# Two output products ended row tile by row tile, and the last layer's input turned, split and first multiplied by tiles

## The reference

```python
def even_layer(x, ...):                    # first layer of the second block
    ...
    y = jnp.concatenate([y_a, y_b], axis=-1) @ w_out        # 256x2048 @ 2048x1024
    return x + rms_norm_2(y, g_post)

def odd_layer(x, ...):                     # last layer
    h = rms_norm_2(x, g_pre)
    p = h @ w_in                                            # 256x1024 @ 1024x2752
    c_q, c_kv, k_r, f_in, z_c, z_d = split_cols(p, ODD_SIZES)   # 384, 256, 64, 512, 1024, 512
    ...
    y = jnp.concatenate([y_c, y_d], axis=-1) @ w_out        # 256x1536 @ 1536x1024
    return x + rms_norm_2(y, g_post)
```

## Time and profile before

| | |
|---|---|
| median of 3 runs | 870.31 us (868.88 to 870.93) |
| the profiled execution | 870.27 us, span 868.5 us |
| mean granted TensorE clock | 0.997 |
| busy share of the span | PE 98%, PE weight loads 80%, VectorE 58%, ScalarE 55%, GpSimd 4% |
| weights and other reads | 138.56 MB, 161 GB/s over the span |

### The profile page before, as it was taken

One profiled execution on the slowest core, in us unless ns is written; L12 is line 12 of the kernel. 1 busy time (PEld: TensorE's weight loads), 2 busy tenths in 40 slices (PEclk: granted clock), 3 DMA queues, 4 the chain that ended last, 5 costly groups with the idle time before them and its releaser, 6 DMA issues.

```text
span 868.5 us, 10829 instructions
## 1 busy us (share of the span) xinstructions
PE 850.9 (98%) x4078; PEld 695.5 (80%) x4078; DVE 500.8 (58%) x759; ACT 476.6 (55%) x761; POOL 38.5 (4%) x67
## 2 busy tenths in 40 slices
PE   8999899999999999999999999999999999999996
PEld 6888787888888888887788766888888887788885
DVE  6657642656666666545355644856665566546463
ACT  6557645663456555433466463438764577555551
POOL 2000000000000000810000010000000100000000
PEclk9999999999999999999999999999999999999999
DMA  8763433655466565675456514535564557265021
GB/s 270 257 190 117 146 97 98 193 172 188 129 197 216 175 186 191 175 240 189 152 178 200 169 33 162 170 98 170 171 219 155 145 171 248 73 184 192 2 97 48
DMA packets 75876, 140.36 MB, mean 162 GB/s; under 512 B 6082, under 2 KB 12517, under 8 KB 75825
## 3 DMA queue, kind: packets, MB, share of 16 engines
q1 hardware_dynamic: 72432, 134.37, 49.2%
q0 software_dynamic: 3328, 5.29, 2.2%
q10 hardware_dynamic: 64, 0.02, 0.0%
HBM read 138.56 MB, written 1.06 MB: 161 GB/s over the span
## 4 chain that ended last, share of the span: by engine, by line
PE 90%; DVE 4%; ACT 3%; issue 1%; DMA 1%; SPq 0%; DVEq 0%; ACTq 0%
PE acc L1552 25%; PE acc L1554 25%; PE acc L1553 25%; PE aux L1588 2%; PE aux L1840 2%; PE aux L1905 1%; DVE wlo L388 1%; ACT whi L534 1%; PE aux L2024 1%; PE aux L1968 1%; PE aux L1829 1%; DMA raw<-in_w_in 1%; PE aux L2032 1%; PE aux L2033 1%; PE aux L1701 1%
## 5 line engine op out<-in xcount | busy, mean ns | idle before, releaser
L388 DVE TENSOR_TENSOR wlo<-raw,whi 128x1024 fp32r<-128x1024 f32 (+2 forms) x257 | 304.7, 1203 | 228.6 <-ACT whi L534 227.9
L534 ACT ACTIVATE whi<-raw 128x1024 fp32r<-128x1024 f32 (+2 forms) x257 | 264.4, 1045 | 232.6 <-PE acc L1554 208.9
L1552 PE MATMUL acc<-whi,a_hi 128*128 128x512 f32 (+4 forms) x720 | 277.5, 385 | 3.3 <-DVE wlo L388 2.5
L1554 PE MATMUL acc<-whi,a_lo 128*128 128x512 f32 (+4 forms) x720 | 272.7, 379 | 0.0
L1553 PE MATMUL acc<-wlo,a_hi 128*128 128x512 f32 (+4 forms) x720 | 272.2, 378 | 0.0
L1552 PEld LDWEIGHTS acc<-whi,a_hi 128*128 128x128 f32 x720 | 135.8, 189 | 33.0 <-issue 5.4
L1554 PEld LDWEIGHTS acc<-whi,a_lo 128*128 128x128 f32 x720 | 135.6, 188 | 24.9
L1553 PEld LDWEIGHTS acc<-wlo,a_hi 128*128 128x128 f32 x720 | 135.8, 189 | 24.2 <-issue 0.7
L1552 PE MATMUL acc<-whi,b_hi 128*128 128x512 f32 x234 | 92.3, 395 | 0.1
L1554 PE MATMUL acc<-whi,b_lo 128*128 128x512 f32 x234 | 91.2, 390 | 0.0
L1553 PE MATMUL acc<-wlo,b_hi 128*128 128x512 f32 x234 | 91.1, 389 | 0.0
(11 more groups left out here) (334 smaller groups left out, 774.6 us busy)
## 6 DMA issues: line engine op xcount, KB each, us to landing
raw<-in_even_w_in SPq DMA_DIRECT2D x54, 512.0 KB, 4.4
raw<-in_w_in SPq DMA_DIRECT2D x50, 512.0 KB, 3.8
raw<-in_w_up SPq DMA_DIRECT2D x32, 512.0 KB, 4.5
raw<-in_w_down SPq DMA_DIRECT2D x32, 512.0 KB, 3.5
raw<-in_even_w_out SPq DMA_DIRECT2D x16, 512.0 KB, 4.1
raw<-in_odd_w_in SPq DMA_DIRECT2D x16, 512.0 KB, 4.5
raw<-in_odd_w_out SPq DMA_DIRECT2D x12, 512.0 KB, 3.7
raw<-in_w_branch_gla SPq DMA_DIRECT2D x8, 512.0 KB, 3.3
```

Source lines behind the costliest of these rows:

```text
L388: return e.tensor_tensor(w_view(wlo[u % SPLIT], u), w_view(raw[u % RAW], u), w_view(whi[u % SPLIT], u).bitcast(F32), ALU.subtract)
L534: act.activation(w_view(whi[u % SPLIT], u), w_view(raw[u % RAW], u), ACT.Copy).then_inc(sem("hi_done"), 1)
L1552: pe.matmul(acc_of(c, t), ah[:, ts], hi[:, k], start=first, stop=False)
L1554: ins = pe.matmul(acc_of(c, t), al[:, ts], hi[:, k], start=False, stop=last)
```

## The change

Each tile of 128 tokens ends on its own. PE takes E1 to E4 for tile 0 (12 + 12 matmuls) and then for tile 1, with the turning of H's tile 0 (`turn_input(0)`, 8 transposes into two banks) between E3 and E4 of tile 1. Then it takes all of oq for tile 0, turns tile 1, takes K1 for tile 0, oq for tile 1, K2 and K3 for tile 0 and okv for tile 1. The idle turns are gone. ScalarE and VectorE get new functions that do one tile or one bank at a time (`row_squares`, `row_rstd`, `input_hi`, `times_gain`, `add_normed`, `input_lo`), and the making of Q1 to Q4 is put between them by hand. A wait of `norm_stats(3)` is now by tile. In the last product the units 2 to 5 of oy1 are taken for tile 0 and then for tile 1, with its sums, adds and stores by tile.

```diff
--- before.py
+++ after.py
@@ -158,7 +158,7 @@
             AUX += [("num", h, d, t) for h in range(4) for d in range(2) for t in range(2)]
             AUX += split_keys("eh", 8) + split_keys("ea", 8)
         if STAGES >= 3:
-            AUX += split_keys("on", 8) + split_keys("cq", 3) + split_keys("ckv", 2) + [("krT",)]
+            AUX += [("tr", "on", t, j) for t in range(NT) for j in range(2)] + split_keys("cq", 3) + split_keys("ckv", 2) + [("krT",)]
             AUX += [("dft", g) for g in range(4)] + split_keys("fr", 4) + [("knT", j) for j in range(4)]
             AUX += [("qnT", j) for j in range(4)] + [("qrT", j) for j in range(2)]
             for h in range(8):
@@ -413,6 +413,16 @@
             hi, lo, o = WHERE[name]
             return hi[:, o + k], lo[:, o + k], key
 
+        def act_key(name, k, tiles):
+
+            return ("tr", name, tiles[-1], k // 4) if name == "on" else act_tile(name, k)[2]
+
+        SQUARES = [[(0, 0), (1, 0), (0, 1), (1, 1)], [(0, 0), (0, 1), (1, 0), (1, 1)]]
+
+        def square_count(i, n, t):
+
+            return 4 * i + SQUARES[i].index((n, t)) + 1
+
         def halves(key):
             return bank(key)[:, :].rearrange("p (k t) -> p k t", k=2)
 
@@ -431,9 +441,9 @@
                 dst = raw[u % RAW][:, 0:nk * nn].rearrange("p (k n) -> p k n", k=nk)
                 src = w[k * P:(k + nk) * P, n0:n0 + nn].rearrange("(k p) n -> p k n", p=P)
                 sp.dma_start(dst, src).then_inc(sem(f"raw_in{u % RAW}"), 16)
-            for n in range(2):
-                for t in range(NT):
-                    sp.wait_ge(sem("h_out"), 2 * NT * (STAGES - 2) + NT * n + t + 1)
+            for t in range(NT):
+                for n in range(2):
+                    sp.wait_ge(sem("h_out"), 2 * NT * (STAGES - 2) + 2 * t + n + 1)
                     sp.dma_start(out[0, t * P:(t + 1) * P, 512 * n:512 * n + 512], H[:, t, 512 * n:512 * n + 512]
                                  ).then_inc(sem("stored"), 16)
             sp.wait_ge(sem("stored"), 16 * 2 * NT)
@@ -726,22 +736,28 @@
                     aux_free(ins, key)
             pump("dn1", 3)
             if STAGES >= 2:
...
+                def row_squares(c, i, n, t):
+                    use("natural_log_exp_and_others")
+                    acc_wait(act, f"{c}{n}", t)
+                    own = square_count(i, n, t)
+                    if own > 2:
+                        act.wait_ge(sem("y_squared"), own - 2)
+                    act.activation(junk[:, 512 * (own % 2):512 * (own % 2) + 512], acc_of(f"{c}{n}", t), ACT.Square,
+                                   accum_out=ystat[:, i, t, n:n + 1]).then_inc(sem("y_squared"), 1)
+
+                def row_rstd(i, t):
+                    act.wait_ge(sem("y_squared"), square_count(i, 1, t))
+                    chain(act.activation(yrms[:, i, t:t + 1], ystat[:, i, t, 0:1], ACT.Identity, bias=ystat[:, i, t, 1:2]))
+                    rstd(yrms[:, i, t:t + 1], D).then_inc(sem("y_rstd"), 1)
+
+                def input_hi(t, j):
+                    key = ("tr", "on", t, j)
+                    aux_wait(act, key)
+                    for i in range(4):
+                        k = 4 * j + i
+                        ins = act.activation(a_hi[:, k, P * t:P * t + P], bank(key)[:, P * i:P * i + P], ACT.Copy,
+                                             scale=gain("opre", k))
+                    ins.then_inc(sem("hi_split"), 1)
 
                 def dn_done(t):
                     for n in range(2):
@@ -870,11 +886,22 @@
                 split_hi("ea", range(4))
                 pump("ez1", 11)
                 split_hi("ea", range(4, 8))
-                post_norm("ey", 0)
+                pump("ey1", 1)
+                row_squares("ey", 0, 0, 0)
+                row_squares("ey", 0, 1, 0)
+                row_rstd(0, 0)
+                pump("ey1", 2)
+                row_squares("ey", 0, 0, 1)
+                pump("ey1", 3)
+                input_hi(0, 0)
+                input_hi(0, 1)
+                pump("ey1", 4)
+                row_squares("ey", 0, 1, 1)
+                row_rstd(0, 1)
+                input_hi(1, 0)
+                input_hi(1, 1)
             if STAGES >= 3:
-                split_hi("on", range(4), lambda k: gain("opre", k))
-                split_hi("on", range(4, 8), lambda k: gain("opre", k))
-                norm_stats(3, lambda t: act.wait_ge(sem("h_out"), 2 * NT))
+                norm_stats(3, lambda t: act.wait_ge(sem("h_out"), 2 * t + 2))
                 for w, (c, n) in enumerate((("oq", 384), ("okv", 256))):
                     pump(c)
                     for t in range(NT):
@@ -959,7 +986,13 @@
                 turned(7)
                 split_hi("yd", range(4))
                 split_hi("yc", range(8))
-                post_norm("oy", 1)
+                pump("oy0")
+                for t in range(NT):
+                    row_squares("oy", 1, 0, t)
+                pump("oy1")
+                for t in range(NT):
+                    row_squares("oy", 1, 1, t)
+                    row_rstd(1, t)
 
 
         @block.vector
@@ -1370,33 +1403,49 @@
                 pump("ez1", 11)
                 split_lo("ea", range(4, 8))
 
...
+                def times_gain(c, n, t, i, g, tmp):
+
+                    dve.wait_ge(sem("post_in"), 16 * (i + 1))
+                    dve.wait_ge(sem("y_squared"), square_count(i, n, t))
+                    cs = slice(512 * n, 512 * n + 512)
+                    acc_free(dve.tensor_tensor(tmp[:, t, cs], acc_of(f"{c}{n}", t), g[:, cs], ALU.mult), f"{c}{n}")
+
+                def add_normed(c, t, i, tmp):
+
+                    dve.wait_ge(sem("y_rstd"), 2 * i + t + 1)
                     for n in range(2):
                         cs = slice(512 * n, 512 * n + 512)
-                        for t in range(NT):
-                            acc_done(dve, f"{c}{n}", t)
-                            dve.scalar_tensor_tensor(out=H[:, t, cs], in0=tmp[:, t, cs], scalar=yrms[:, i, t:t + 1],
-                                                     in1=H[:, t, cs], op0=ALU.mult, op1=ALU.add
-                                                     ).then_inc(sem("h_out"), 1)
-
-                for n in range(2):
-                    pump(f"ey{n}")
-                    times_gain("ey", n, 0, post_g, YTMP)
-                add_normed("ey", 0, YTMP)
+                        acc_done(dve, f"{c}{n}", t)
+                        dve.scalar_tensor_tensor(out=H[:, t, cs], in0=tmp[:, t, cs], scalar=yrms[:, i, t:t + 1],
+                                                 in1=H[:, t, cs], op0=ALU.mult, op1=ALU.add
+                                                 ).then_inc(sem("h_out"), 1)
+
+                def input_lo(t, j):
+                    key = ("tr", "on", t, j)
+                    aux_wait(dve, key)
+                    dve.wait_ge(sem("hi_split"), SPLITS[key] + 1)
+                    for i in range(4):
+                        k, ts = 4 * j + i, slice(P * t, P * t + P)
+                        ins = dve.scalar_tensor_tensor(out=a_lo[:, k, ts], in0=bank(key)[:, P * i:P * i + P],
+                                                       scalar=gain("opre", k), in1=a_hi[:, k, ts].bitcast(F32),
+                                                       op0=ALU.mult, op1=ALU.subtract)
+                    aux_free(ins, key)
+
+                pump("ey1", 1)
+                times_gain("ey", 0, 0, 0, post_g, YTMP)
+                times_gain("ey", 1, 0, 0, post_g, YTMP)
+                add_normed("ey", 0, 0, YTMP)
+                pump("ey1", 2)
+                times_gain("ey", 0, 1, 0, post_g, YTMP)
+                input_lo(0, 0)
+                pump("ey1", 3)
+                input_lo(0, 1)
+                pump("ey1", 4)
+                times_gain("ey", 1, 1, 0, post_g, YTMP)
+                add_normed("ey", 1, 0, YTMP)
+                input_lo(1, 0)
+                input_lo(1, 1)
             if STAGES >= 3:
-                split_lo("on", range(4), lambda k: gain("opre", k))
-                split_lo("on", range(4, 8), lambda k: gain("opre", k))
                 pump("oq")
 
                 C1, C2, C3 = TWO_PI
@@ -1518,32 +1567,36 @@
                 split_lo("yc", range(8))
                 for n in range(2):
                     pump(f"oy{n}")
-                    times_gain("oy", n, 1, post2, YTMP2)
-                add_normed("oy", 1, YTMP2)
+                    for t in range(NT):
+                        times_gain("oy", n, t, 1, post2, YTMP2)
+                        if n == 1:
+                            add_normed("oy", t, 1, YTMP2)
 
 
         @block.tensor
         def _(pe):
             done = [0]
 
-            def product(c, n0=0, n1=None):
+            def product(c, n0=0, n1=None, tiles=range(NT)):
 
 
                 i, ch = CI[c], CH[CI[c]]
-                if i >= 2 and n0 == 0:
+                if i >= 2 and n0 == 0 and tiles[0] == 0:
```

(61 more changed lines are left out.)

## The result

| | before | after |
|---|---|---|
| median | 870.40 us (868.88 to 870.93, 6 runs) | 874.76 us (871.91 to 875.56, 6 runs) |
| the profiled execution | 870.27 us, span 868.5 | 871.91 us, span 870.2 |
| mean granted TensorE clock | 0.997 | 0.993 |

The ratio is 1.0036, with a 95% interval of 1.0020 to 1.0052: about 3.1 us slower, where 873.5 us (+3.2) had been forecast. A second set, taken with the experiments, has 875.08 against 871.18, ratio 1.0047 (1.0034 to 1.0060). The profiled execution is the fastest of its six.

What follows compares the result with a forecast made beforehand. PE was taken as the bound, with time lost where it stands still. F2 later +2.86, slow clock +1.9 and the end -1.55 summed to +3.2 on 870.27: 873.5 us, with an 8-in-10 range of 870.8 to 875.8.

Steps and rivals of the forecast that it cites:

- Tile 0, no wait at the first turning: At the seam, H's tile 0 is ready at 685.25, before PE comes at 686.18; PE then waits 0.8 us for bank 0.
- Tile 1: At the seam, VectorE finishes tile 1's adds at 693.95; PE waits 0.6 us, then turns tile 1 from 694.0 to 694.9.
- The narrow copies: Splits of a bank at the seam: four 128x128 ScalarE copies of 0.25 us each, 1.1 us a bank.
- K1: After tile 1's turns: K1's weights come behind norm_stats(3), so PE waits 7.0 us, from 694.9 to 701.9.
- From K1 to F2: From K1's start to F2 14.85 us, decided by the angles; F2 starts at 716.75, 2.86 us later than before.
- The clock: At K1, after the 7.0 us gap: PE starts at 1.2 GHz, which loses 1.9 us; bounds nothing and twice that.
- The end: End of the program: one row's factor and two adds remain after the last matmul, -1.55 us; bounds -1.2 and -1.7.
- last rival: At the seam, K1 is ready when PE has turned tile 1; F2 at 712.2, the end at 867.0 us; chance 5%.
- only a third of the seam: What the rival with K1 ready would gain at the seam, F2 1.7 us earlier, as the angles' chain holds F2.
- the angles' chain: Between F1's low part and F2: angles, table load, sine and F2's own split, 7.85 us as before, said to hold F2.

Runs made afterwards that it cites:

- one place: The changed kernel with K1's weights made between the copies of tile 1 and norm_stats; ratio 1.0003 to the kernel before (871.66 against 871.88 us).
- the idle turns: The changed kernel with 58 turns of nothing (6.3 us) put between the turning of tile 1 and K1; ratio 1.0008 to the kernel before.
- the end alone: The kernel before with only the change's last product, sums, adds and stores by tile; 870.21 against 871.88 us, ratio 0.9981.
- second profile: The changed kernel, unchanged, profiled and timed again beside the experiments; ratio 1.0047 to the kernel before (875.08 against 871.18 us).
- K1 no filler: The changed kernel with PE's order alone altered, oq's tile 1 ahead of K1; 867.84 against 871.18 us before, ratio 0.9964.
- K1 and then F2 made early: The changed kernel with K1 made before tile 1's copies, then also F2's weights made before the angles; ratios to before 0.9959, then 0.9935.
- K1 made early: The changed kernel with ScalarE and VectorE making K1's weights before the copies of tile 1; 867.19 us, ratio 0.9959 to the kernel before.

## Why the prediction was right

Step by step, in the prediction's own terms:

- **Tile 0, no wait at the first turning.** Right: no wait in the row at 685.16. Bank 0's wait was put at 0.8 and is 0.74. The table load (1.28 us) lies under E1 and E2, at 676.76.
- **Tile 1.** A wait of 0.6 before the second turning was expected, 0.19 is shown; yet that turning comes 7.76 us behind the first, where 7.8 was worked out. The prediction counted waits from where the next matmul could be issued. Counted so, the two waits are 0.9 and 0.4 where it had 0.8 and 0.6.
- **The narrow copies.** 8 of them take 2.17 us, a pitch of 0.26, where 0.25 was taken from the row. The estimate by the rule of the Trainium skill (ScalarE: Activation LUTs, "What ACT_TABLE_LOAD costs") was 0.29. The measurement decides: the row was the better guide.
- **K1.** 15.7 us behind the turning was predicted (701.9 - 686.18), and 15.72 is measured in two profiles. The gap of 7.0 is 6.88, or 7.1 counted from where the next matmul could be issued. That it is norm_stats and the missing `pump` is shown by moving K1's making (2.7 us by one place, all of the gap by the other) and by taking K1 out of the way.
- **From K1 to F2.** At full clock +2.86 was summed, +2.94 is measured with the idle turns.
- **The clock.** 1.9 us; measured 1.32 and 2.55, and by the times possibly more. It did fall, but that the size lies between the two is luck: how the clock falls and comes back was read off one event each and does not repeat: 4.4 us after the last matmul in the earlier trace rows, 2 to 3 us after it at the seam; back after 3.9 us in the earlier trace rows, after 2.9 and 5.5 here.
- **The end.** -1.55; measured -1.54 in the profile, and 1.7 us in the times of the end alone.

The sum for the profiled execution: 4.26 at the seam less 1.54 is +2.7, and its E1 starts 1.0 us earlier than in the profile of before, +1.7; 870.2 - 868.5 = 1.7. The second profile's first turning stands at 686.18, level with before, and its sum is 5.49 - 1.57 = +3.9: its span is 872.4, 3.9 longer, and the times of that set show +4.1 (1.0047). That the first set's ratio gives +3.1 us where +3.2 was forecast is luck: its medians differ by 4.4, the second set's ratio gives +4.1, and the two profiles +1.7 and +3.9. The range of 870.8 to 875.8 held, thanks more to its bounds than to the term for the clock.

The prediction's last rival, that the gain arrives, put F2 1.7 us earlier than before, "only a third of the seam". K1 no filler has the chain that it describes and gains 1.16. But with K1 and then F2 made early the seam gives 2.38 and 3.47 us, so the angles' chain was no fixed bound: it too hung on where the weights are made.

Where the seam begins differs by up to 4 us between executions of the same work (first turnings at 685.16 to 689.32): in the profiles of K1 made early, K1 no filler and the end alone the granted clock has a mean of 0.93 between 500 and 550 us, in that of before 0.97, in the two of the changed kernel 1.00. That is not all of it, for the latest of them, with the idle turns, has 0.97 there; the rest is open. That part of the program is untouched, which is why the measures above count from the turning.

## What to carry to other kernels

A filler is only one if its inputs are ready: before putting an instruction into a wait on an in-order engine, find in each producer's own program what stands ahead of the work that it needs. Here the filler's weights stood behind the very chain that it should have covered, and as PE takes its units in order, it stopped the pipeline of weights as well. And when a stretch of idle work is taken out, ask whether the gap is gone too; if it isn't, the clock's fall may be paid on top, as it was here.

## What the hardware showed beyond that

The clock fell after less idleness than the prediction's single row suggested. It went to 1.2 GHz 3.0 us (697.0 against 694.0), 2.2 us (697.2 against 695.0) and 2.8 us (698.3 against 695.5) after the end of the last turning, and once though PE had stood still for only 2.12 us (windows of the kernel in which K1 is no filler):

```profile
698.00:700.00 2.00, 0.72 (x4) 1.00 0.74 37
700.00:702.00 2.00, 2.00 (x10) 0.63 0.82 320
702.00:703.00 1.00, 1.00 (x5) 0.50 1.00 377
703.00:704.00 1.00, 1.00 (x5) 0.52 0.27 107
704.00:705.00 1.00, 1.00 (x7) 1.00 0.06 8
```

PE takes up its work at 699.28, and the mean of 0.63 over 700 to 702 puts the fall at 700.5, when PE has been busy again for 1.2 us; it is back at 704.0. PE had waited three times in the 9 us before (0.74, 0.19 and 2.12 us). In the changed kernel, with the same first two waits, the fall came within the third, of 6.88 us. With K1 made early, where the third wait is 0.55 us, the clock is 1.00 in all windows of the seam, as in these two:

```profile
698.00:700.00 2.00, 1.46 (x10) 1.00 0.83 187
700.00:702.00 2.00, 2.00 (x14) 1.00 0.93 109
```

What decides between these cases, and whether PE has 2.9 or 5.5 us of work at the low level after its gap, these runs don't settle.
